# Attention's inverse sums as a scaled identity in a product, and two more weight pieces summed by VectorE

## The chip, the cores and the metric

One core of one Trainium2 chip. The metric is device microseconds of one execution. Below, PE is TensorE's matmuls, PEld its weight loads, DVE is VectorE, ACT ScalarE, POOL GpSimd and SP SyncE.

## The reference

Two layers of a diffusion backbone on 256 latent tokens of width 2048, with 256 context tokens. Layer 0 mixes by attention (16 heads of 128, 4 key heads), layer 1 by a Fourier transform; an MLP follows each. What matters here is layer 0's attention and the vectors from c that scale and shift:

```python
mod_lat = (silu_c @ ada_w[i] + ada_b[i])[:, None, :]
sh1, sc1, g1, sh2, sc2, g2 = jnp.split(mod_lat, N_MOD, axis=-1)
...
logits = jnp.concatenate([
    jnp.einsum('bqkgd,bskd->bkgqs', q, k_lat),
    jnp.einsum('bqkgd,bskd->bkgqs', q, k_ctx)], axis=-1).astype(jnp.float32) * scale
p = jax.nn.softmax(logits, axis=-1).astype(v_lat.dtype)
return (jnp.einsum('bkgqs,bskd->bqkgd', p[..., :s], v_lat)
        + jnp.einsum('bkgqs,bskd->bqkgd', p[..., s:], v_ctx))
...
x = x + g2 * sq_relu_mlp(modulate(rms_norm(x, norm_mlp_g[i]), sh2, sc2), mlp_w1[i], mlp_w2[i])
```

## The kernel before

The program is written out by hand for each engine: each engine's queue runs in the order of the code, and semaphores tie the queues. Weights come from HBM in pieces of 1 MB on SP's queue; ScalarE makes the high part of each slice (w_hi, L727) and VectorE the low part (w_lo, L1201), and a product with them is three matmuls (L1848 to L1850). This is done LOOKAHEAD = 4 slices ahead of TensorE.

**The attention loop** is the loop over n = 0 to 37 on each of three engines. Tile n is head n // 2 and token half n % 2, so there are 32 tiles of 128 queries by 512 keys. In step n TensorE issues, in this order: the score of tile n + 1 (L2204, one f32 product of 512 columns); from n = 6 a unit of the output projection W_o (block_unit, L1848 to L1850); an early piece, if the step has one (L1933); for m = n - 1 the four transposes of prob (L2242); at even n from 4 the four products of v with probT, for both tiles of head (n - 4) // 2 (L2257); and at n = 1, 3, 7, 9, 11 and 13 the turns of q_acc (L1963), which wait for VectorE's rotation of these heads (q_epilogue). VectorE takes the maximum of each score (L1523), then, with the exponent's sum from ScalarE (L937), inverts the sum (L1529) and multiplies the 128x512 tile prob by it (L1530), for tile m = n - 1. TensorE transposes the result, ScalarE copies it to probT (L926). Behind the products ScalarE and VectorE split the head's output in a high (L948) and a low part (h_lo, L1544) for block_unit. ScalarE also copies the turned heads to qT (L842).

**The early pieces.** The vector products silu(c) times ada_w for the first MLP's shift (v = 1, pieces j = 0 to 15) and scale (v = 2, j = 16 to 31) are done piece by piece, 1 MB each, from a ring of buffers that POOL's queue fills (load_vector, i = j + 16). A piece is either a group of four matmuls into bank 2 by TensorE (early_piece) or two halves of a running sum by VectorE (early_sum, L1505 for the first piece, L1508 for the rest). EARLY_TENSOR and EARLY_VECTOR say which. At the end early_fold adds VectorE's sum into the same bank. Of the scale vector's 16 pieces TensorE has j = 17 (at n = 25) and j = 19 (at n = 27). The vector sums of v = 2 begin at n = 23 with piece 16, and go on in the output projection behind the loop, at slice i of LATE_SUMS. A load may start once the piece that was in its buffer is used (before_early), and POOL's queue issues loads strictly in order.

Of the kernel before, what the change touches and what calls it, by code (L numbers as in the profile page):

```python
# [22 lines left out]
F32 = mybir.dt.float32  # L23
F32R = mybir.dt.float32r
ALU = mybir.AluOpType
# [3 lines left out]
P = 128  # L29
# [121 lines left out]
def early_slot(j):  # L151
# [1 line left out]
    return (4, 5, 7, 2, 7, 2, 10, 10, 0, 2, 1, 8, 0, 9, 1, 8)[j] if j < 16 else (9, 0, 8, 1)[j % 4]  # L153


EARLY_TENSOR = ((0, 1, 2, 3, 4, 5, 6, 7, 8, 10, 12, 14), (17, 19))
EARLY_VECTOR = ((9, 11, 13, 15), (16, 18, 20, 22, 24, 26, 28, 21, 23, 30, 25, 27, 29, 31))
LATE_SUMS = {3: ((21, 0), (21, 1)), 4: ((23, 0),), 5: ((23, 1),), 6: ((30, 0),), 7: ((30, 1),), 8: ((25, 0),), 11: ((25, 1),),
             12: ((27, 0),), 13: ((27, 1),), 14: ((29, 0),), 15: ((29, 1),), 16: ((31, 0),), 19: ((31, 1),)}


# [15 lines left out]
def vector_halves(j):  # L177

    return 2 * (EARLY_VECTOR[0] + EARLY_VECTOR[1]).index(j) + 2

# [64 lines left out]
def layer_block(nc, x, c, ctx_in, c_ctx, ada_w, ada_b, norm_mix_g, norm_mlp_g, w_qkv, q_g, k_g, w_o,  # L245
# [4 lines left out]
    def place(name, shape, dt, at):  # L250
        return nc.alloc_sbuf_tensor_at(name, shape, dt, offset=at)
# [11 lines left out]
    shared = base[0]  # L263
# [62 lines left out]
    probT = place("probT", [P, 2, 4, T], F32, shared + 24576)  # L326
    prob = place("prob", [P, 3, 2 * T], F32, shared + 32768)
    nmax = place("nmax", [P, 32, 4], F32, shared + 38912)
    sum_front = place("sum_front", [P, D], F32, shared)
    sum_down = place("sum_down", [P, D], F32, shared + 36864)  # L330

# [205 lines left out]
    def turned_bank(m):  # L537
        return 3 if m >= 5 and m % 2 else 6
# [101 lines left out]
    @block.gpsimd  # L640
    def _(pool):
        def load_start(n):

            if n >= 7:
                pool.wait_ge(ada_mm, n - 2)
            if n == 4:
                pool.wait_ge(ctx_rows_in, 16)
            if n < 8:
                dst, src = ring(start_slot(n)).rearrange("p (k c) -> p k c", k=8), first_v[n // 4, n % 4 // 2, n % 2]
            else:  # L650
                dst, src = ring(start_slot(n)).rearrange("p (k c) -> p k c", k=4), start_v[n // 8, n % 8 // 4, n % 4]
            pool.dma_start(dst, src).then_inc(ada_in[start_slot(n)], 16)

        def load_vector(i):

            lay, m = SUMS[i // KT]
            if i < 2:
                pool.wait_ge(prod_done, 32)
            elif i == 8:
                pool.wait_ge(ada_mm, 32)  # L660
            elif i == 9:
                pool.wait_ge(ada_mm, 30)
            elif i < 16:
                pool.wait_ge(ada_used, i - 1)
            elif i < 18:
                pool.wait_ge(prod_done, 64)
            elif i == 18:
                pool.wait_ge(ada_used, 7)
            elif i == 19:
                pool.wait_ge(ada_mm, 31)  # L670
            elif i < 22:
                pool.wait_ge(ada_mm, tensor_count(i - 18))
            elif i == 22:
                pool.wait_ge(prod_done, 80)
            elif i == 23:
                pool.wait_ge(ada_mm, tensor_count(6))
            elif i in (24, 26):
                pool.wait_ge(ada_used, 15 + (i - 24) // 2)
            elif i == 25:
                pool.wait_ge(ada_mm, tensor_count(5))  # L680
            elif i in (27, 29):
                pool.wait_ge(head_T, 11 + (i - 27) // 2)
            elif i < 50:
                j = before_early(i - 16) if i < 48 else 29 + 2 * (i - 48)
                if j in EARLY_VECTOR[j // KT]:
                    pool.wait_ge(early_used, vector_halves(j))
                else:
                    pool.wait_ge(ada_mm, tensor_count(j))
            else:
                pool.wait_ge(ada_used, i - 33)  # L690
            if i in (9 * KT, 9 * KT + 1):
                pool.wait_ge(slice_done, 2 * P_DOWN[0] - QKV + 128)
            pool.dma_start(ring(vector_slot(i)), ada_v[lay][m, i % KT]).then_inc(ada_in[vector_slot(i)], 16)  # L693

        for n in range(19):
            load_start(n)
        load_vector(0)
        load_vector(1)
        for a in range(6):
            load_start(19 + 2 * a)  # L700
            load_start(20 + 2 * a)
            load_vector(2 + a)
        load_start(31)
        for i in (8, 9, 16, 17, 10, 11, 18, 12, 19, 20, 21, 13, 14, 22, 23, 15):
            load_vector(i)
        for i in (*range(24, 41), 42, 44, 46, 41, 43, 45, *range(47, 160)):
            load_vector(i)


# [486 lines left out]
    def _(dve):  # L1196
# [322 lines left out]
        for n in range(38):  # L1519
            if n < 32:  # L1520
                h, tt = n // 2, n % 2
                dve.wait_ge(score_ready, n + 1)
                step(nc.vector.tensor_reduce(nmax[:, n, 0:1], ps[:, 4 + n % 2, :], AX_X, ALU.max))  # L1523
                nc.vector.scalar_tensor_tensor(nmax[:, n, 1:2], nmax[:, n, 0:1], -1.0, q_rs[:, h, tt:tt + 1], ALU.mult,
                                               ALU.mult).then_inc(max_ready, 1)
            m = n - 1
            if 0 <= m < 32:
                dve.wait_ge(exp_ready, m + 1)
                step(nc.vector.reciprocal(nmax[:, m, 3:4], nmax[:, m, 2:3]))  # L1529
                nc.vector.tensor_scalar(prob[:, m % 3, :], prob[:, m % 3, :], nmax[:, m, 3:4], None, ALU.mult).then_inc(prob_ready, 1)  # L1530
            if n in (1, 2, 4):
                add_product(76 + (1, 2, 3)[n // 2])
            if n == 16:
                gate_add(0, 7)
            if n in WOVEN_SPLITS:
                split_lo(QKV + WOVEN_SPLITS.index(n))
            if n == 0:
                ada_step(0, 11)
            if n in ROTATE_AT:
                q_epilogue(1 + ROTATE_AT.index(n) // 2, ROTATE_AT.index(n) % 2)  # L1540
            if n >= 5 and n % 2 == 1 and n < 37:
                h = (n - 5) // 2
                dve.wait_ge(o_hi_ready, h + 1)
                nc.vector.tensor_tensor(h_lo[:, h, :], ps[:, 7, 0:T], h_hi[:, h, :].bitcast(F32), ALU.subtract).then_inc(o_ready, 1)  # L1544
            if n in (1, 3, 6, 10):
                ada_step(0, 12 + (1, 3, 6, 10).index(n))
            if n == 7:
                dve.wait_ge(q_root, 2)
                step(nc.vector.reciprocal(q_rs[:, 4:16, :], q_rs[:, 4:16, :]))
            if n == 24:  # L1550
                take_early(1)
            if 13 <= n < 21 or 23 <= n < 37:
                early_sum((9 if n < 21 else 6) + (n - 13) // 2 * 2, (n - 13) % 2)
        split_lo(59)

# [287 lines left out]
    def _(pe):  # L1843
# [80 lines left out]
        def early_piece(j):  # L1924

            slot, v = vector_slot(16 + j), j // KT
            pe.wait_ge(ada_in[slot], 16 * vector_count(16 + j))
            if j == 0:
                pe.wait_ge(acc_add, 45)
            if j == EARLY_TENSOR[1][0]:  # L1930
                pe.wait_ge(early_ready, 1)
            for b in range(4):
                ins = mm(ps[32 * b:32 * b + 32, 2, :], silu[:, j % KT, :], ring(slot)[:, 512 * b:512 * (b + 1)],  # L1933
                         start=(j == EARLY_TENSOR[v][0]), stop=False, skip_group_check=True)
            ins.then_inc(ada_mm, 1)

        def early_fold(v):

            pe.wait_ge(early_used, vector_halves(EARLY_VECTOR[v - 1][-1]))
            total = (spare[7], ada_sum)[v - 1]  # L1940
            for b in range(4):
                ins = mm(ps[32 * b:32 * b + 32, 2, :], ones[:, 0:32], total[:, 512 * b:512 * (b + 1)], start=False, stop=True,
                         skip_group_check=True)
            ins.then_inc(ada_mm, 1)

# [262 lines left out]
        for n in range(38):  # L2208
# [18 lines left out]
                early_fold(1)  # L2227
            if n == 23:
                early_cols(1)
            if n in (25, 27):  # L2230
                early_piece(n - 8)
            m = n - 1
            if 0 <= m < 32:
                pe.wait_ge(prob_ready, m + 1)
                if m >= 5:
                    pe.wait_ge(probT_out, m - 1)
                elif m >= 1:
                    pe.wait_ge(probT_out, m)
                else:
                    pe.wait_ge(head_T_out, 5)  # L2240
                for st in range(4):
                    ins = nc.tensor.transpose(ps[:, turned_bank(m), st * P:(st + 1) * P], prob[:, m % 3, st * P:(st + 1) * P], ident[:, :])  # L2242
                ins.then_inc(probT_ready, 1)
            if n == 15:
                pe.wait_ge(o_ready, 6)
# [209 lines left out]
```

## Time and profile before

| what | before |
|---|---|
| median of 3 runs | 2003.79 us (2003.05 to 2006.21) |
| the profiled execution, its own time | 2005.52 us |
| its span | 2003.6 us |
| TensorE busy | 1965.9 us |
| VectorE busy | 1391.5 us |
| ScalarE busy | 969.3 us |

The span runs from the first to the last instruction of the profiled execution; its own time is 1.9 us longer. Busy times overlap. The attention loop lies between about 250 and 376 us of the span, and the output projection W_o between 376 and 437.

### The profile page before, as it was taken

The page shows a single profiled execution, that of the slowest core. Times are in us where ns is not written, and L with a number is a line of the kernel's source. Part 1 is how long each engine was busy: PE and PEld are TensorE (multiplying, and loading weights), DVE is VectorE, ACT ScalarE, POOL GpSimd, SP SyncE. Part 2 cuts the span into 40 slices and gives each one's busy share as a digit, 9 for nine tenths or more (in the row PEclk, how much of TensorE's full clock was granted, in tenths as well). Part 3 has the DMA queues.
Part 4 walks back from the last instruction along what each step waited for, and adds up shares of the span by engine and source line. Part 5 has one row for each costly group of instructions (what it writes and reads, how often), then busy time and mean ns, then how long its engine had stood idle before and what let it go on. Part 6 is the DMA issues. An engine that isn't in the chain of part 4 may idle for free.

```text
span 2003.6 us, 24992 instructions
## 1 busy us (share of the span) xinstructions
PE 1965.9 (98%) x10188; PEld 1609.5 (80%) x10188; DVE 1391.5 (69%) x1424; ACT 969.3 (48%) x1265; POOL 110.9 (6%) x196
## 2 busy tenths in 40 slices
PE   6999989999999999999999999999999999999998
PEld 4677756778888888888888888788888888888886
DVE  3666998889867787788888675766666455555556
ACT  6432565455544455544444464555554454444444
POOL 1111001000000000000000000000000000000000
PEclk9999999999999999999999999999999999999999
DMA  9998768779989899799999626577776566555653
GB/s 359 338 378 319 277 257 297 272 252 323 353 293 348 313 360 364 262 367 363 355 395 383 219 85 193 175 252 253 257 251 220 187 192 210 189 192 198 218 190 126
DMA packets 152261, 542.80 MB, mean 271 GB/s; under 512 B 9393, under 2 KB 10577, under 8 KB 114641
## 3 DMA queue, kind: packets, MB, share of 16 engines
q1 hardware_dynamic: 119312, 335.77, 47.9%
q0 software_dynamic: 31744, 201.34, 27.1%
q10 hardware_dynamic: 1090, 4.09, 0.5%
q8 instruction: 81, 1.33, 0.3%
q14 instruction: 34, 0.28, 0.0%
HBM read 535.91 MB, written 2.10 MB: 269 GB/s over the span
## 4 chain that ended last, share of the span: by engine, by line
PE 94%; DVE 3%; ACT 1%; DMA 1%; issue 1%; POOL 0%; ACTq 0%; DVEq 0%; POOLq 0%
PE ps L2098 13%; PE ps L2036 12%; PE ps L2032 12%; PE ps L2035 11%; PE ps L2096 11%; PE ps L2099 6%; PE ps L1848 6%; PE ps L2095 6%; PE ps L1849 5%; PE ps L1850 5%; PE ps L2257 1%; PE ps L1913 1%; PE ps L2204 1%; DMA spare<-in_ada_w 1%; PE ps L2242 1%
## 5 line engine op out<-in xcount | busy, mean ns | idle before, releaser
L1201 DVE TENSOR_TENSOR w_lo<-raw,w_hi 128x1024 fp32r<-128x1024 f32 x616 | 749.5, 1223 | 467.9 <-ACT w_hi L727 467.6
L727 ACT ACTIVATE w_hi<-raw 128x1024 fp32r<-128x1024 f32 x616 | 649.4, 1059 | 845.7 <-PE ps L2036 345.8
L2098 PE MATMUL ps<-hh,w_hi 128*128 128x512 f32 x1088 | 427.5, 398 | 1.1 <-DVE hh L1627 1.1
L2032 PE MATMUL ps<-w_hi,hh 128*128 128x512 f32 x992 | 385.9, 389 | 0.0
L2036 PE MATMUL ps<-w_hi,hh 128*128 128x512 f32 x992 | 385.9, 389 | 0.0
L2035 PE MATMUL ps<-w_lo,hh 128*128 128x512 f32 x992 | 385.9, 389 | 0.0
L2096 PE MATMUL ps<-hh,w_hi 128*128 128x512 f32 x960 | 379.9, 396 | 0.0
L2099 PE MATMUL ps<-hh,w_lo 128*128 128x256 f32 x1088 | 302.9, 278 | 0.0
L2095 PE MATMUL ps<-hh,w_lo 128*128 128x256 f32 x960 | 267.5, 279 | 0.0
L2099 PEld LDWEIGHTS ps<-hh,w_lo 128*128 128x128 f32 x1088 | 205.7, 189 | 40.9
L2035 PEld LDWEIGHTS ps<-w_lo,hh 128*128 128x128 f32 x992 | 186.2, 188 | 38.9
L2032 PEld LDWEIGHTS ps<-w_hi,hh 128*128 128x128 f32 x992 | 186.2, 188 | 38.5
L2036 PEld LDWEIGHTS ps<-w_hi,hh 128*128 128x128 f32 x992 | 186.2, 188 | 38.4
L2098 PEld LDWEIGHTS ps<-hh,w_hi 128*128 128x128 f32 x1088 | 207.2, 190 | 11.2 <-issue 5.0
L2095 PEld LDWEIGHTS ps<-hh,w_lo 128*128 128x128 f32 x960 | 180.2, 188 | 43.7
L1229 DVE SCALAR_TENSOR_TENSOR ada_sum<-ada_raw,silu,ada_sum 128x2048 f32<-128x2048 f32 x83 | 194.7, 2346 | 2.7 <-DMA ada_raw<-in_ada_w 2.6
L1848 PE MATMUL ps<-w_hi,hh 128*128 128x512 f32 x448 | 190.8, 426 | 3.5 <-DVE hh L1351 1.6
L2096 PEld LDWEIGHTS ps<-hh,w_hi 128*128 128x128 f32 x960 | 179.9, 187 | 0.0
L1849 PE MATMUL ps<-w_lo,hh 128*128 128x512 f32 x448 | 175.8, 392 | 0.0
L1850 PE MATMUL ps<-w_hi,hh 128*128 128x512 f32 x448 | 175.2, 391 | 0.0
L693 POOL DMA_DIRECT2D ada_raw<-in_ada_w x132 | 70.5, 534 | 1138.3 <-DVE ada_sum L1229 584.3
L1848 PEld LDWEIGHTS ps<-w_hi,hh 128*128 128x128 f32 x448 | 84.5, 189 | 39.7 <-issue 14.4
(252 smaller groups left out, 1620.4 us busy)
## 6 DMA issues: line engine op xcount, KB each, us to landing
raw<-in_mlp_w SPq DMA_DIRECT2D x256, 1024.0 KB, 5.3
ada_raw<-in_ada_w POOLq DMA_DIRECT2D x151, 1024.0 KB, 6.2
spare<-in_ada_w POOLq DMA_DIRECT2D x29, 1024.0 KB, 6.6
raw<-in_attn_w_qkv SPq DMA_DIRECT2D x24, 1024.0 KB, 10.1
raw<-in_attn_w_o SPq DMA_DIRECT2D x16, 1024.0 KB, 5.7
raw<-in_fourier_w_o SPq DMA_DIRECT2D x16, 1024.0 KB, 5.1
g_row<-in_ada_w POOLq DMA_DIRECT2D x12, 1024.0 KB, 9.0
g_row<-gate_rows SPq DMA_DIRECT2D x48, 64.0 KB, 5.2
```

The lines of the kernel that those rows point to most:

```text
L727: act.activation(w_slot(s)[0], raw[:, piece % RAW, s % 2, :], ACT.Copy).then_inc(hi_ready, 1)
L1201: nc.vector.tensor_tensor(lo, raw[:, s // 2 % RAW, s % 2, :], hi.bitcast(F32), ALU.subtract).then_inc(lo_ready, 1)
L1848: mm(dst, w_h, m_h, start=start, stop=False, skip_group_check=True)
L1849: mm(dst, w_h, m_l, start=False, stop=False, skip_group_check=True)
L1850: return mm(dst, w_l, m_h, start=False, stop=stop, skip_group_check=True)
L2032: ins = mm(bank_of(tt, nb), h_hi[:, k % KT, tok], hi[:, cols], start=start, stop=False)
L2035: mm(bank_of(tt, nb), h_hi[:, k % KT, tok], lo[:, cols], start=False, stop=False)
L2036: return mm(bank_of(tt, nb), h_lo[:, k % KT, tok], hi[:, cols], start=False, stop=stop)
L2095: mm(ps[:, bank, 0:T], w_lo[:, s % SPLIT, w], h_hi[:, k, :], start=False, stop=False, skip_group_check=True)
L2096: ins = mm(both, w_hi[:, s % SPLIT, w], hh[:, k, :, :], start=False, stop=(k == KT - 1), skip_group_check=True)
L2098: mm(both, w_hi[:, s % SPLIT, w], hh[:, k, :, :], start=(k == 0), stop=False, skip_group_check=True)
L2099: ins = mm(ps[:, bank, 0:T], w_lo[:, s % SPLIT, w], h_hi[:, k, :], start=False, stop=(k == KT - 1), skip_group_check=True)
```

## The change

The tile prob is no longer multiplied by the inverse sums. VectorE instead multiplies the 128x128 identity by them (a diagonal matrix, `inverse`, three buffers), and TensorE's transpose of prob becomes a product of prob with that diagonal matrix, which turns and scales in one. The second part gives pieces 17 and 19 to VectorE, so that TensorE has no piece of the scale vector. Piece 17 is the first of that vector's sums, at n = 21 and 22; piece 19 is summed at slice 0 of W_o, behind the first split there. early_fold(2) starts its bank in place of piece 17, and waits for early_ready, as that piece did. On POOL's queue the load of j = 23 moves behind that of j = 30, since its buffer is now free only after piece 19's sum.

```diff
-EARLY_TENSOR = ((0, 1, 2, 3, 4, 5, 6, 7, 8, 10, 12, 14), (17, 19))
-EARLY_VECTOR = ((9, 11, 13, 15), (16, 18, 20, 22, 24, 26, 28, 21, 23, 30, 25, 27, 29, 31))
-LATE_SUMS = {3: ((21, 0), (21, 1)), ...
+EARLY_TENSOR = ((0, 1, 2, 3, 4, 5, 6, 7, 8, 10, 12, 14), ())
+EARLY_VECTOR = ((9, 11, 13, 15), (17, 16, 18, 20, 22, 24, 26, 28, 19, 21, 23, 30, 25, 27, 29, 31))
+LATE_SUMS = {0: ((19, 0), (19, 1)), 3: ((21, 0), (21, 1)), ...
...
+    inverse = place("inverse", [P, 3, P], F32, shared + 39424)
...
-        for i in (*range(24, 41), 42, 44, 46, 41, 43, 45, *range(47, 160)):
+        for i in (*range(24, 39), 40, 42, 44, 46, 39, 41, 43, 45, *range(47, 160)):
             load_vector(i)
...
-                nc.vector.tensor_scalar(prob[:, m % 3, :], prob[:, m % 3, :], nmax[:, m, 3:4], None, ALU.mult).then_inc(prob_ready, 1)
+                nc.vector.tensor_scalar(inverse[:, m % 3, :], ident[:, :], nmax[:, m, 3:4], None, ALU.mult).then_inc(prob_ready, 1)
...
-            if 13 <= n < 21 or 23 <= n < 37:
+            if n in (21, 22):
+                early_sum(17, n - 21)
+            elif 13 <= n < 37:
                 early_sum((9 if n < 21 else 6) + (n - 13) // 2 * 2, (n - 13) % 2)
...
-            if j == EARLY_TENSOR[1][0]:
-                pe.wait_ge(early_ready, 1)
...
             pe.wait_ge(early_used, vector_halves(EARLY_VECTOR[v - 1][-1]))
+            if v == 2:
+                pe.wait_ge(early_ready, 1)
...
-                ins = mm(ps[32 * b:32 * b + 32, 2, :], ones[:, 0:32], total[:, 512 * b:512 * (b + 1)], start=False, stop=True,
+                ins = mm(ps[32 * b:32 * b + 32, 2, :], ones[:, 0:32], total[:, 512 * b:512 * (b + 1)], start=(v == 2), stop=True,
...
-            if n in (25, 27):
-                early_piece(n - 8)
...
-                    ins = nc.tensor.transpose(ps[:, turned_bank(m), st * P:(st + 1) * P], prob[:, m % 3, st * P:(st + 1) * P], ident[:, :])
+                    ins = mm(ps[:, turned_bank(m), st * P:(st + 1) * P], prob[:, m % 3, st * P:(st + 1) * P], inverse[:, m % 3, :],
+                             start=True, stop=True)
```

How the order moves shows best in a few rows. First TensorE at n = 25 and 26, before: score, W_o unit, piece 17, four transposes, and the next step.

```order
L2204 MATMUL ps<-kT,qT 128x512
L1848 MATMUL ps<-w_hi,hh 128x512
L1849 MATMUL ps<-w_lo,hh 128x512
L1850 MATMUL ps<-w_hi,hh 128x512
L1933 MATMUL ps<-ada_raw,silu 32x512 x4
L2242 MATMUL ps<-ident,prob 128x128 x4
L2204 MATMUL ps<-kT,qT 128x512
L1848 MATMUL ps<-w_hi,hh 128x512
L1849 MATMUL ps<-w_lo,hh 128x512
L1850 MATMUL ps<-w_hi,hh 128x512
L2242 MATMUL ps<-ident,prob 128x128 x4
L2257 MATMUL ps<-probT,v_acc 128x256 x4
```

The same steps of the changed kernel, whose lines have moved by one to three:

```order
L2207 MATMUL ps<-kT,qT 128x512
L1851 MATMUL ps<-w_hi,hh 128x512
L1852 MATMUL ps<-w_lo,hh 128x512
L1853 MATMUL ps<-w_hi,hh 128x512
L2243 MATMUL ps<-inverse,prob 128x128 x4
L2207 MATMUL ps<-kT,qT 128x512
L1851 MATMUL ps<-w_hi,hh 128x512
L1852 MATMUL ps<-w_lo,hh 128x512
L1853 MATMUL ps<-w_hi,hh 128x512
L2243 MATMUL ps<-inverse,prob 128x128 x4
L2259 MATMUL ps<-probT,v_acc 128x256 x4
```

The piece (L1933) is gone, and what turned prob with ident now multiplies it with inverse. VectorE before, from the multiply of prob at n = 21 on, through n = 22:

```order
L1530 TENSOR_SCALAR prob<-prob,nmax 128x512
L1201 TENSOR_TENSOR w_lo<-raw,w_hi 128x1024
L1544 TENSOR_TENSOR hh<-ps,hh 128x256
L1523 TENSOR_REDUCE nmax<-ps 128x1
L1524 SCALAR_TENSOR_TENSOR nmax<-nmax,q_rs 128x1
L1529 RECIPROCAL nmax<-nmax 128x1
L1530 TENSOR_SCALAR prob<-prob,nmax 128x512
L1201 TENSOR_TENSOR w_lo<-raw,w_hi 128x1024
L1523 TENSOR_REDUCE nmax<-ps 128x1
```

And in the changed kernel:

```order
L1531 TENSOR_SCALAR inverse<-ident,nmax 128x128
L1202 TENSOR_TENSOR w_lo<-raw,w_hi 128x1024
L1545 TENSOR_TENSOR hh<-ps,hh 128x256
L1506 TENSOR_SCALAR ada_sum<-ada_raw,silu 128x1024
L1524 TENSOR_REDUCE nmax<-ps 128x1
L1525 SCALAR_TENSOR_TENSOR nmax<-nmax,q_rs 128x1
L1530 RECIPROCAL nmax<-nmax 128x1
L1531 TENSOR_SCALAR inverse<-ident,nmax 128x128
L1202 TENSOR_TENSOR w_lo<-raw,w_hi 128x1024
L1506 TENSOR_SCALAR ada_sum<-ada_raw,silu 128x1024
L1524 TENSOR_REDUCE nmax<-ps 128x1
```

The two halves of piece 17 (L1506) stand behind the h_lo of n = 21 and behind the split of n = 22. VectorE at the beginning of W_o before, from the splits of slices 59 to 61 on:

```order
L1201 TENSOR_TENSOR w_lo<-raw,w_hi 128x1024 x3
L1575 TENSOR_TENSOR gated_120<-ps,g_row 128x512
L1578 TENSOR_TENSOR x_tm<-x_tm,gated_120 128x512
L1201 TENSOR_TENSOR w_lo<-raw,w_hi 128x1024
L1575 TENSOR_TENSOR gated_120<-ps,g_row 128x512
```

And in the changed kernel:

```order
L1202 TENSOR_TENSOR w_lo<-raw,w_hi 128x1024 x2
L1509 SCALAR_TENSOR_TENSOR ada_sum<-ada_raw,silu,ada_sum 128x1024 x2
L1202 TENSOR_TENSOR w_lo<-raw,w_hi 128x1024
L1578 TENSOR_TENSOR gated_121<-ps,g_row 128x512
L1581 TENSOR_TENSOR x_tm<-x_tm,gated_121 128x512
L1202 TENSOR_TENSOR w_lo<-raw,w_hi 128x1024
```

The two halves of piece 19 (L1509) stand between the splits of slices 60 and 61.

## Rows read from the trace of the kernel before

**Rows 1.** The page: busy time, and the chain that ended last by engine.
```profile
PE 1965.9 (98%) x10188; PEld 1609.5 (80%) x10188; DVE 1391.5 (69%) x1424; ACT 969.3 (48%) x1265; POOL 110.9 (6%) x196
...
PE 94%; DVE 3%; ACT 1%; DMA 1%; issue 1%; POOL 0%; ACTq 0%; DVEq 0%; POOLq 0%
```
**Rows 2.** Windows: stretch, its length, busy us of each engine (instructions), granted clock, DMA.
```profile
249.70:267.80 18.10, 18.01 (x92) 10.95 (x91) 17.72 (x29) 10.32 (x37) 2.41 (x5) 1.00 0.79 291
267.80:300.20 32.40, 27.16 (x136) 16.99 (x135) 30.92 (x61) 22.48 (x61) 2.90 (x6) 1.00 0.64 235
300.20:361.20 61.00, 60.96 (x304) 39.61 (x303) 50.30 (x104) 34.48 (x72) 8.05 (x14) 1.00 0.83 301
361.20:376.00 14.80, 13.38 (x61) 9.77 (x60) 12.64 (x21) 6.93 (x14) 1.58 (x3) 1.00 0.63 231
378.00:434.00 56.00, 56.00 (x249) 46.37 (x248) 49.67 (x48) 25.26 (x33) 2.64 (x5) 1.00 0.83 290
```
**Rows 3.** Groups by shape, 249.7 to 376: count, busy us, mean ns, idle before.
```profile
L2204 PE MATMUL ps<-kT,qT 128*128 128x512 f32 x64 | 32.9, 596 | 0.0
L2257 PE MATMUL ps<-probT,v_acc 128*128 128x256 f32 x128 | 30.3, 379 | 0.0
...
L2257 PEld LDWEIGHTS ps<-probT,v_acc 128*128 128x128 f32 x128 | 23.1, 190 | 2.6
...
L2242 PE MATMUL ps<-ident,prob 128*128 128x128 f32 x128 | 20.0, 279 | 3.5 <-ACT probT L926 2.5 <-DVE prob L1530 0.8
...
L1530 DVE TENSOR_SCALAR prob<-prob,nmax 128x512 f32<-128x512 f32 x32 | 15.6, 486 | 1.1
...
L1505 DVE TENSOR_SCALAR ada_sum<-spare,silu 128x1024 f32<-128x1024 f32 x2 | 1.5, 747 | 0.0
```
**Rows 4.** The chain in order of time: start, us on the chain, what.
```profile
340.70 0.79 PE ps L1951 x8
...
350.38 0.44 PE ps L2242 x4
350.82 1.73 PE ps L2257 x8
352.55 0.86 PE ps L2204 x2
```
**Rows 5.** Waits of TensorE, 255 to 300.2: us in total, times, longest.
```profile
PE ps L2242 <- ACT probT L926: 2.5, 1, 2.5
PE ps L1963 <- issue: 2.4, 2, 1.3
```
**Rows 6.** Timeline of ScalarE at the end of n = 3: start, us, idle before.
```profile
268.04 0.60 ACT L842 ACTIVATE qT<-ps 128x512 f32<-128x512 f32 x1 [0.88 <-PE ps L1963]
```
**Rows 7.** Timeline of TensorE: the scores that begin n = 27 to 30.
```profile
352.38 1.02 PE L2204 MATMUL ps<-kT,qT 128*128 128x512 f32 x2
...
355.52 1.02 PE L2204 MATMUL ps<-kT,qT 128*128 128x512 f32 x2
...
359.25 1.02 PE L2204 MATMUL ps<-kT,qT 128*128 128x512 f32 x2
...
361.24 1.02 PE L2204 MATMUL ps<-kT,qT 128*128 128x512 f32 x2
```
**Rows 8.** POOL's timeline (load of piece 17), and its loads' median landing, 230 to 460.
```profile
325.64 0.69 POOL L693 DMA_DIRECT2D ada_raw<-in_ada_w  x1
...
ada_raw<-in_ada_w POOLq DMA_DIRECT2D x18, 1024.0 KB, 7.2
```
**Rows 9.** Timeline of VectorE at n = 21.
```profile
333.48 0.42 DVE L1544 TENSOR_TENSOR hh<-ps,hh 128x256 fp32r<-128x256 f32 x1
```
**Rows 10.** Timeline of VectorE in W_o: first split, and piece 23's first half.
```profile
380.86 1.23 DVE L1201 TENSOR_TENSOR w_lo<-raw,w_hi 128x1024 fp32r<-128x1024 f32 x1 [0.97 <-ACT w_hi L727]
...
393.70 1.28 DVE L1508 SCALAR_TENSOR_TENSOR ada_sum<-ada_raw,silu,ada_sum 128x1024 f32<-128x1024 f32 x1
```
**Rows 11.** Waits of TensorE, 300.2 to 376.
```profile
PE ps L2242 <- DVE prob L1530: 0.8, 1, 0.8
```

More of the change, by code:

```diff
@@ L153, in early_slot @@
     return (4, 5, 7, 2, 7, 2, 10, 10, 0, 2, 1, 8, 0, 9, 1, 8)[j] if j < 16 else (9, 0, 8, 1)[j % 4]
-EARLY_TENSOR = ((0, 1, 2, 3, 4, 5, 6, 7, 8, 10, 12, 14), (17, 19))
-EARLY_VECTOR = ((9, 11, 13, 15), (16, 18, 20, 22, 24, 26, 28, 21, 23, 30, 25, 27, 29, 31))
-LATE_SUMS = {3: ((21, 0), (21, 1)), 4: ((23, 0),), 5: ((23, 1),), 6: ((30, 0),), 7: ((30, 1),), 8: ((25, 0),), 11: ((25, 1),),
+EARLY_TENSOR = ((0, 1, 2, 3, 4, 5, 6, 7, 8, 10, 12, 14), ())
+EARLY_VECTOR = ((9, 11, 13, 15), (17, 16, 18, 20, 22, 24, 26, 28, 19, 21, 23, 30, 25, 27, 29, 31))
+LATE_SUMS = {0: ((19, 0), (19, 1)), 3: ((21, 0), (21, 1)), 4: ((23, 0),), 5: ((23, 1),), 6: ((30, 0),), 7: ((30, 1),), 8: ((25, 0),), 11: ((25, 1),),
              12: ((27, 0),), 13: ((27, 1),), 14: ((29, 0),), 15: ((29, 1),), 16: ((31, 0),), 19: ((31, 1),)}
```

## The prediction, written before the changed kernel was run

> **What bounds the kernel now.** I began with the page. TensorE is busy for 98% of the span, and of the chain of work that ended last 94% is TensorE and 3% VectorE [rows 1]: a microsecond of TensorE's work is nearly always one of the span, unless it falls where TensorE waits. The change lies in the attention loop and behind it, so I cut that part into stretches. From 249.7 to 267.8 us (n = 0 to 3) TensorE is idle for 0.09 us, from 267.8 to 300.2 (n = 4 to 11) for 5.24, from 300.2 to 361.2 (n = 12 to 29) for 0.04, in the tail up to 376 for 1.42, and in W_o (378 to 434) for nothing. VectorE is idle for 1.9 us in the first two stretches, 10.7 in the third and 6.3 in W_o [rows 2]. So the loop has a first part in which VectorE, ScalarE and TensorE wait for each other, and a long second part that TensorE alone paces.
>
> Then I read the operations by shape. The 128 transposes of prob (32 tiles of 4) have 128 records. The 32 score products have 64, and the 64 products of prob and v have 128 [rows 3]: an ordinary f32 product is two records, a transpose is one. A record's mean duration (279 to 596 ns) is latency, since records overlap, so I took the pace from the chain in order of time: four transposes 0.44 us, eight records of probT times v (256 columns) 1.73, two of a score (512 columns) 0.86, eight with only 4 columns 0.79 [rows 4]. That is 0.11, 0.216 and 0.43 us per record for 128, 256 and 512 columns, in proportion, and a floor of 0.10 for a record whose columns are few but whose weights are a full 128x128.
>
> **The change part by part.**
>
> *Product in place of transpose, on TensorE.* Each of the 32 tiles issues four f32 products of 128 columns, with prob as weights and the scaled identity moving. By the count of records that is eight in place of four. By columns each takes 0.11, and the floor for full weights is no higher, so a tile costs 8 x 0.11 = 0.88 against 0.44: **+0.44**. The bounds are 0 (were it one record, as now) and +1.08 (were the weight load, 0.19 us for such products [rows 3], not overlapped: 8 x 0.19 - 0.44). The eight 4-column records also load full weights and take 0.79 in all, which puts it near the lower of the two.
>
> The Trainium skill speaks against the change here: FP8 and Floating Point Precision, TensorE Precision Notes, has true fp32 as four passes, and TensorE: Matmul & The Clock Gate, Terms, calls transpose mode 4x faster for FP32. The trace has a factor of two between transpose and product of equal columns, and the measurement decides.
>
> *First part, n = 1 to 11, 11 tiles.* They add 11 x 0.44 = 4.84 us to TensorE, and what counts is which of its waits they fill. These are 2.5 us for ScalarE's probT at n = 4, 2.4 us in two waits ahead of the turns of q_acc at n = 7 and 11 (for VectorE's rotation) [rows 5], and 0.3 that are left of the 5.24 idle, at n = 6. The first fills nothing: ScalarE reaches that copy only after one of qT for which it waited 0.88 us on TensorE's turns at the end of n = 3 [rows 6], so TensorE's delay goes round through ScalarE and comes back. The others (2.7) are filled, for TensorE arrives at them some 2 us late and VectorE does not. That leaves 4.84 - 2.7 = **+2.1**. The bounds: +4.84 if nothing is filled, and -2.4 if VectorE alone sets the pace there and its gain (below) is all that counts, 12 steps of 0.2.
>
> *VectorE's product.* The 128x512 tensor_scalar (0.486 us, 32 times) becomes 128x128, which the trace doesn't have. Between 128x512 and 128x1024 (0.747) [rows 3] the slope is 0.51 ns a column, which gives 0.29. The bounds are 0.49 (no gain) and 0.12 (a quarter of the present time, in proportion to the columns). I take 0.29: 0.2 less a step, 6.4 in all. In the second part this is worth nothing, for TensorE does not wait there.
>
> *Second part, n = 12 to 28, 17 tiles.* 17 x 0.44 = **+7.5**, hidden by nothing.
>
> *Pieces 17 and 19.* Between the starts of the scores lie 3.14 us at n = 27, which has a piece, and 1.99 at n = 29, the same step without one [rows 7]. So a piece is 1.15, and two are **-2.3**. Their sums go to VectorE: two halves at n = 21 and 22 (as the first of the vector they are tensor_scalar at 0.75, and piece 16's become the dearer form, about 1.28, as the sum at 393.70 [rows 10]), and two of 1.28 behind the first split of W_o. In the loop that is +2.6 us against 10.7 of idle, and 3.6 saved there; in W_o it is +2.6 against 6.3. Behind the new sums queue the next splits, for which TensorE would wait, but they are made several slices ahead; without that cover the 2.6 would be on the path.
>
> Piece 17 must land earlier now. It is issued at 325.64 and the median landing takes 7.2 us, so it is there near 332.9 [rows 8]; the sum wants it when the h_lo of 333.48 is done [rows 9], at 333.8 to 333.9. The tiles of the three steps between give about 1 us more. I cost it at nothing; were it 2 us late, VectorE's idle time would hide half and it would cost 1. On POOL's queue piece 23's load now waits for piece 19's second half, near 384.6 (380.86 + 1.2 + 2.5), and lands 7.2 later, near 391.8; its sum comes at 393.70 or after [rows 10], so it is in time.
>
> *Tail, n = 29 to 32, 4 tiles.* Here prob of the last tile comes 0.8 us after TensorE wants it [rows 11], behind an early sum. The four tiles add 1.8; that wait, less the 0.2 that VectorE is earlier, and a share of the other idle time of this stretch (1.42 in all) take 1.0 of it: **+0.8**.
>
> Sum: 2.1 + 7.5 - 2.3 + 0.8 = +8.1 us. The profiled execution took 2005.52 (span 2003.6), so it would take 2013.6. It lies 1.7 over the median of the runs, on which I put the forecast: 2003.79 + 8.1 = **2011.9 us**, slower by 0.4%. Everything behind the loop is paced by TensorE and only shifts.
>
> **The rivals.**
> - *A. The product runs at the transpose's pace*, one record each. For it: same shape and an identity as moving operand. Against it: every other f32 product has two records. Then TensorE gets nothing, the pieces give -2.3, the first part -1.6 through VectorE and the tail -0.2: -4.1, 1999.7 us, faster. It decides when the extra of a tile is below about 0.1 us.
> - *B. VectorE paces the first part.* For it: it is idle for only 1.9 of 50.5 us there. Against it: TensorE's idle time is in a few waits, and n = 8 to 10 have hardly any. -2.4 instead of +2.1: +3.6, 2007.4, at the edge of no change.
> - *C. The weight load is not overlapped*: 1.08 a tile, 0.64 over my price on the 28 tiles that count: +18 more, 2030. Against it: the 4-column row.
> - *D. A product is four times a transpose*: 1.76 a tile instead of 0.88, 0.88 more on 28 tiles: +25, 2037. Against it: the score's 0.86 for 512 columns is 1.68 ns a column, twice the transpose's 0.86. The skill's 4x (TensorE: Matmul & The Clock Gate, Terms) would be this case.
>
> **How the numbers follow.** Mine 0.78, B 0.08, A 0.07, C 0.04, D 0.03. A difference under 0.2% (4.0 us) is about what a measurement of this kernel can't tell from none. Faster is A, 0.07; within 0.2% are B and a corner of mine, 0.10; slower is the rest, 0.83. Mine alone spans +5 to +11.7 (waits of the first part and of the tail filled or not: +2.8 and +1.0 above the sum; more filled, 3 below it). With B's edge the range is 2007.0 to 2015.5.
>
> **What would show it.** 256 records for the product, with chain pieces of 0.87 to 0.90 us for eight; scores 2.4 us apart at n = 25, 27 and 29, and 4.2 at the even steps; the wait for probT at n = 4 still there, those ahead of the turns of q_acc gone; W_o without idle time on TensorE; VectorE's product near 0.29. I am wrong if the product has 128 records, if n = 12 starts no later than 300.2, or if VectorE waits for ada_raw at n = 21.

## The result, and the profile after

| what | before | after |
|---|---|---|
| median, timed side by side | 2004.53 us (4 runs, 2003.05 to 2006.21) | 2014.45 us (4 runs, 2013.59 to 2015.39) |
| the profiled execution, its own time | 2005.52 us | 2014.73 us |
| its span | 2003.6 us | 2012.6 us |

The changed kernel is slower: ratio 1.0048, 95% interval 1.0036 to 1.0061, that is 7 to 12 us, about 9.6. The forecast was 2011.9 us in a range of 2007.0 to 2015.5.

First the page of the changed kernel, busy time and the chain by engine (before in [rows 1]):

```profile
PE 1977.1 (98%) x10300; PEld 1625.7 (81%) x10300; DVE 1390.0 (69%) x1428; ACT 970.7 (48%) x1265; POOL 110.0 (5%) x196
...
PE 95%; DMA 3%; DVE 1%; ACT 0%; issue 0%; POOL 0%; SPq 0%; ACTq 0%; DVEq 0%; POOLq 0%
```

TensorE has 112 records more (128 for the product, less 16 of the two pieces) and 11.2 us more busy time. VectorE's busy time is nearly the same: what its short product saves, the four new half sums take.

The windows of the changed kernel, cut at the same steps as [rows 2] (n = 0 to 3, 4 to 11, 12 to 28, tail, W_o; same columns):

```profile
249.20:268.50 19.30, 19.30 (x104) 12.54 (x103) 18.91 (x30) 10.30 (x37) 2.51 (x5) 1.00 0.74 273
268.50:302.80 34.30, 31.80 (x169) 22.50 (x167) 28.62 (x63) 22.83 (x61) 2.62 (x5) 0.95 0.60 222
302.80:367.20 64.40, 64.40 (x347) 46.77 (x346) 46.90 (x100) 33.97 (x70) 6.84 (x13) 1.00 0.73 263
367.20:384.70 17.50, 16.79 (x85) 13.14 (x85) 13.71 (x23) 7.96 (x16) 1.59 (x3) 1.00 0.63 228
387.00:443.00 56.00, 56.00 (x248) 46.39 (x248) 51.65 (x50) 25.38 (x32) 3.17 (x6) 1.00 0.86 303
```

From n = 12 on TensorE is idle for nothing up to the tail, as before, and W_o has no idle time either. New is the granted clock of 0.95 in the second row.

Where the time came: between the first score of the loop (249.17) and the last product of v (382.69) lie 133.52 us, before 124.31 (249.67 to 373.98). The loop has 9.2 us more. Everything behind it nearly only shifts: the transposes of x behind W_o start 8.68 us later than before, TensorE's last product 9.04 (2003.38 and 1994.34).

Groups by shape in the loop (count, busy us, mean ns, idle before; before in [rows 3]):

```profile
L2243 PE MATMUL ps<-inverse,prob 128*128 128x128 f32 x256 | 35.7, 284 | 2.7 <-ACT probT L927 2.5 <-DVE inverse L1531 0.2
L2243 PEld LDWEIGHTS ps<-inverse,prob 128*128 128x128 f32 x256 | 33.4, 195 | 12.9 <-issue 9.7 <-DVE inverse L1531 1.5
...
L1531 DVE TENSOR_SCALAR inverse<-ident,nmax 128x128 f32<-128x128 f32 x32 | 9.2, 287 | 1.1
```

256 records stand where the transpose had 128. The chain in order of time gives their pace, as [rows 4] did:

```profile
296.27 0.89 PE ps L2243 x8
297.16 1.73 PE ps L2259 x8
298.89 0.86 PE ps L2207 x2
```

Eight records take 0.89 us, 0.45 more than the four of the transpose. The scores that begin n = 25 to 29 (before in [rows 7]) are 2.45, 4.17, 2.45, 4.18 us apart:

```profile
354.00 1.02 PE L2207 MATMUL ps<-kT,qT 128*128 128x512 f32 x2
356.45 1.02 PE L2207 MATMUL ps<-kT,qT 128*128 128x512 f32 x2
360.62 1.02 PE L2207 MATMUL ps<-kT,qT 128*128 128x512 f32 x2
363.07 1.02 PE L2207 MATMUL ps<-kT,qT 128*128 128x512 f32 x2
367.25 1.02 PE L2207 MATMUL ps<-kT,qT 128*128 128x512 f32 x2
```

All of TensorE's waits from 250 to 310 (before in [rows 5]): the one for probT is left, those ahead of the turns of q_acc are gone.

```profile
PE ps L2243 <- ACT probT L927: 2.5, 1, 2.5
```

And its waits from 310 to 390 (before in [rows 11]): the 0.8 us for prob is down to 0.2.

```profile
PE ps L1851 <- DVE hh L1545: 0.5, 2, 0.2
PE ps L2243 <- DVE inverse L1531: 0.2, 1, 0.2
```

VectorE at n = 21: the h_lo, and the first half of piece 17 right behind it. The second row has no wait in brackets, so piece 17 was there. The third row is its load on POOL's queue, which landed 9.2 us later.

```profile
339.29 0.42 DVE L1545 TENSOR_TENSOR hh<-ps,hh 128x256 fp32r<-128x256 f32 x1 [0.30 <-ACT hh L949]
339.63 0.74 DVE L1506 TENSOR_SCALAR ada_sum<-ada_raw,silu 128x1024 f32<-128x1024 f32 x1
...
329.93 0.53 POOL L694 DMA_DIRECT2D ada_raw<-in_ada_w  x1
```

### The profile page after: what moved, and what is told of

Same layout as the page of the kernel before. It is cut to its first block, busy times and chain, and to the rows that moved or that the text cites. A ratio compares the mean times of both kernels' runs of the same rounds, so it can differ in the third digit from the quotient of the medians.

```text
span 2012.6 us, 25224 instructions
## 1 busy us (share of the span) xinstructions
PE 1977.1 (98%) x10300; PEld 1625.7 (81%) x10300; DVE 1390.0 (69%) x1428; ACT 970.7 (48%) x1265; POOL 110.0 (5%) x196
## 4 chain that ended last, share of the span: by engine, by line
PE 95%; DMA 3%; DVE 1%; ACT 0%; issue 0%; POOL 0%; SPq 0%; ACTq 0%; DVEq 0%; POOLq 0%
PE ps L2101 13%; PE ps L2035 11%; PE ps L2038 11%; PE ps L2039 11%; PE ps L2099 11%; PE ps L2102 6%; PE ps L1851 6%; PE ps L1852 6%; PE ps L1853 6%; PE ps L2098 6%; PE ps L2243 2%; PE ps L2259 1%; PE ps L2207 1%; PE ps L1916 1%; DMA g_row<-in_ada_w 1%; DMA c_rows<-in_ctx 1%
## 5 line engine op out<-in xcount | busy, mean ns | idle before, releaser
L2101 PEld LDWEIGHTS ps<-hh,w_hi 128*128 128x128 f32 x1088 | 207.3, 191 | 11.2 <-issue 5.0
L1853 PE MATMUL ps<-w_hi,hh 128*128 128x512 f32 x448 | 174.7, 390 | 0.0
```

What stands on the lines that cost most here:

```text
L1853: return mm(dst, w_l, m_h, start=False, stop=stop, skip_group_check=True)
L2101: mm(both, w_hi[:, s % SPLIT, w], hh[:, k, :, :], start=(k == 0), stop=False, skip_group_check=True)
```

## The experiments

My theory after the result: the whole loss is 0.45 us per tile for the second record of each product, less the waits it fills in the first part and less 2.4 us for the two pieces. The rivals: that moving the pieces brought nothing and the product cost less; that VectorE's shorter product is what fills the waits; and that the 0.95 clock is part of the change.

Each profile was cut at the starts of the scores, as in the prediction: first part from the loop's first score to that of n = 12, second part up to that of n = 29, tail up to the last product of v. The column clock tells whether the granted clock fell in the first part of that profile. Ratios are to the kernel before, timed beside each.

| kernel | first | second | tail | loop | clock | median us | ratio (95%) |
|---|---|---|---|---|---|---|---|
| before | 50.56 | 59.02 | 14.73 | 124.31 | full | 2004.53 | 1 |
| before again (e6) | 50.88 | 59.04 | 14.72 | 124.64 | fell | 2003.79 (1 run) | |
| changed | 53.63 | 64.45 | 15.44 | 133.52 | fell | 2014.45 | 1.0048 (1.0036 to 1.0061) |
| changed again (e10) | 52.13 | 64.45 | 15.45 | 132.03 | full | 2013.61 | 1.0048 (1.0035 to 1.0060) |
| product alone (e1) | 53.77 | 66.83 | 15.43 | 136.03 | fell | 2015.51 | 1.0048 (1.0034 to 1.0061) |
| pieces alone (e2) | 50.90 | 57.74 | 15.46 | 124.10 | fell | 2005.85 | 1.0001 (0.9992 to 1.0009) |
| short VectorE product, transposes kept (e3) | 49.96 | 58.78 | 14.33 | 123.07 | fell | 2003.56 | 0.9985 (0.9976 to 0.9994) |
| changed, pieces 4 and 5 at n = 4 (e4) | 51.85 | 64.46 | 15.43 | 131.74 | full | 2012.22 | 1.0033 (1.0021 to 1.0046) |
| before + both piece moves (e8) | 51.23 | 57.73 | 15.45 | 124.41 | fell | 2005.37 | 0.9997 (0.9988 to 1.0005) |
| before + pieces 4 and 5 at n = 4 (e9) | 50.59 | 59.02 | 14.72 | 124.33 | full | 2006.07 | 1.0002 (0.9993 to 1.0010) |
| one-pass product (e7) | 48.80 | 57.12 | 14.86 | 120.78 | full | 2002.87 | 0.9986 (0.9977 to 0.9995) |
| one-pass, pieces left (e11) | 49.92 | 59.20 | 14.38 | 123.50 | fell | 2003.17 | 0.9984 (0.9975 to 0.9993) |
| one-pass, earlier copy (e12) | 48.78 | 57.12 | 14.85 | 120.75 | full | 2001.91 | 0.9981 (0.9972 to 0.9990) |
| changed, earlier copy (e13) | 50.64 | 64.45 | 15.43 | 130.52 | full | 2011.68 | 1.0035 (1.0022 to 1.0047) |

A step of the second part or the tail repeats from profile to profile within 0.02 us, while the ratios of the medians carry an interval of 1.7 to 2.5 us to either side. So a part's size is read from the traces, and the sign of the whole from the medians.

### One part of the change at a time

**The product alone**: the scaled identity and the product, with pieces 17 and 19 left on TensorE.

```diff
-                nc.vector.tensor_scalar(prob[:, m % 3, :], prob[:, m % 3, :], nmax[:, m, 3:4], None, ALU.mult).then_inc(prob_ready, 1)
+                nc.vector.tensor_scalar(inverse[:, m % 3, :], ident[:, :], nmax[:, m, 3:4], None, ALU.mult).then_inc(prob_ready, 1)
...
-                    ins = nc.tensor.transpose(ps[:, turned_bank(m), ...], prob[:, m % 3, ...], ident[:, :])
+                    ins = mm(ps[:, turned_bank(m), ...], prob[:, m % 3, ...], inverse[:, m % 3, :], start=True, stop=True)
```

> Only the first half of the change: scaled identity and product, with pieces 17 and 19 left to TensorE at n = 25 and 27. Theory 1 (a tile costs TensorE 0.45 us, a piece 1.15): 2.3 us more than the full change, so 11 to 12.5 us over before, with the steps at n = 25 and 27 at 3.6 us between scores instead of 2.45. Rival (the pieces on VectorE cost as much as they save, since its sums delay something): within 1 us of the full change, some 9.5 to 10 over before.

Timeline, the scores that begin n = 25 to 28, 3.64, 4.18 and 3.64 us apart:

```profile
353.66 1.02 PE L2205 MATMUL ps<-kT,qT 128*128 128x512 f32 x2
357.30 1.02 PE L2205 MATMUL ps<-kT,qT 128*128 128x512 f32 x2
361.48 1.02 PE L2205 MATMUL ps<-kT,qT 128*128 128x512 f32 x2
365.12 1.02 PE L2205 MATMUL ps<-kT,qT 128*128 128x512 f32 x2
```

n = 25 and 27 take 1.19 us more each than the 2.45 of the full change, so there the two pieces give 2.4. The second part is 7.81 us longer than before (17 steps of 0.46) and 2.38 longer than with the pieces moved. The medians, 2015.51 and 2014.45, have equal ratios and don't resolve that difference.

**The pieces alone**: the tables, the load order and early_fold as in the change, prob multiplied and transposed as before.

```diff
-EARLY_TENSOR = ((0, 1, ..., 12, 14), (17, 19))
+EARLY_TENSOR = ((0, 1, ..., 12, 14), ())
```

> Only the second half: pieces 17 and 19 summed by VectorE, prob still multiplied in full and transposed. Theory 1: TensorE loses 2 x 1.15 us in a part of the loop that it alone paces, VectorE hides the sums: 2.0 to 2.4 us under before (0.1%). Rival (VectorE without the short product becomes the pace from n = 21 on): between 0 and 1.5 us under before, with new waits of TensorE for prob at n = 22 to 29.

Its scores that begin n = 25 to 29 (n = 28, at 353.64, is left out):

```profile
345.42 1.02 PE L2207 MATMUL ps<-kT,qT 128*128 128x512 f32 x2
347.41 1.02 PE L2207 MATMUL ps<-kT,qT 128*128 128x512 f32 x2
351.64 1.02 PE L2207 MATMUL ps<-kT,qT 128*128 128x512 f32 x2
...
357.85 1.02 PE L2207 MATMUL ps<-kT,qT 128*128 128x512 f32 x2
```

And its wait for prob among TensorE's waits from 310 to 390 (0.8 in [rows 11]):

```profile
PE ps L2243 <- DVE prob L1531: 2.1, 4, 0.8
```

The steps n = 25 and 27 fall to 1.99 as they should (-2.3), but n = 26 and 28 rise from 3.7 to 4.2 (+1.0) and the tail by 0.7: in steps of 1.99 us TensorE catches up with VectorE and waits for prob. Of 2.3 us some 0.5 are left in the trace (124.10 against the 124.64 of the other profile of before with a fallen clock), and nothing that the runs can tell (ratio 1.0001). The pieces are worth 2.3 only where something else slows TensorE, and in this change the product does.

**The short VectorE product with the transposes kept**: VectorE makes `inverse` as in the change, but nothing reads it, and the transposes turn the undivided prob. The output lacks the division by the sums; the time is that of the other operations.

```diff
-                nc.vector.tensor_scalar(prob[:, m % 3, :], prob[:, m % 3, :], nmax[:, m, 3:4], None, ALU.mult).then_inc(prob_ready, 1)
+                nc.vector.tensor_scalar(inverse[:, m % 3, :], ident[:, :], nmax[:, m, 3:4], None, ALU.mult).then_inc(prob_ready, 1)
```

> VectorE makes the scaled identity (128x128), but nothing reads it: TensorE transposes prob as before, so the output lacks the division by the sums. Pieces as before. It takes the product's price away and leaves VectorE's gain. Theory 1: worth something only where TensorE waits for VectorE, that is at n = 7 and 11, at the tail, and n = 20: 1.5 to 3 us under before. Rival B of the prediction (VectorE paces the whole first part): its 12 steps give 2.4, and the tail 0.4 more, and the waits ahead of the turns of q_acc remain. If it paced the loop as a whole: 6.4 under.

Groups of the transposes and of VectorE's product:

```profile
L2243 PE MATMUL ps<-ident,prob 128*128 128x128 f32 x128 | 20.1, 281 | 3.1 <-ACT probT L927 2.5 <-DVE inverse L1531 0.6
...
L1531 DVE TENSOR_SCALAR inverse<-ident,nmax 128x128 f32<-128x128 f32 x32 | 9.2, 287 | 1.1
```

Against the profile of before with a fallen clock: first part -0.92, second -0.26, tail -0.39. The waits ahead of the turns of q_acc are 1.0 us here in place of 1.6. The first part gained less than the 2.4 us that rival B had for it. So VectorE's part of the change is a gain (0.9985, the interval is clear of 1), and what the product adds on TensorE is the distance from here to the product alone: +3.8, +8.05 and +1.1 us by part, 13 in the trace and 12 in the medians (2015.51 - 2003.56).

### The granted clock at n = 4

The 0.95 of the changed kernel's second window comes from one place. The same window of 4 us in three profiles (columns as in [rows 2]), first the changed kernel:

```profile
272.00:276.00 4.00, 3.93 (x15) 3.61 (x16) 2.81 (x8) 3.21 (x13) 0.00 (x0) 0.60 0.02 6
```

The kernel before, in its second profile (e6):

```profile
272.00:276.00 4.00, 4.00 (x13) 2.56 (x12) 3.63 (x10) 3.31 (x16) 0.00 (x0) 0.58 0.00 0
```

The kernel before, in its first:

```profile
272.00:276.00 4.00, 3.89 (x17) 2.32 (x15) 3.86 (x10) 4.00 (x21) 0.00 (x0) 1.00 0.00 0
```

Ahead of it stands the 2.5 us wait for probT. Timeline of TensorE at n = 4 in the changed kernel:

```profile
268.54 1.02 PE L2207 MATMUL ps<-kT,qT 128*128 128x512 f32 x2
272.07 2.04 PE L2243 MATMUL ps<-inverse,prob 128*128 128x128 f32 x8 [2.50 <-ACT probT L927]
273.91 2.56 PE L2259 MATMUL ps<-probT,v_acc 128*128 128x256 f32 x8
276.30 1.02 PE L2207 MATMUL ps<-kT,qT 128*128 128x512 f32 x2
```

The same rows in its second profile (e10), where n = 4 begins at 269.98:

```profile
273.51 1.13 PE L2243 MATMUL ps<-inverse,prob 128*128 128x128 f32 x8 [2.51 <-ACT probT L927]
274.48 1.89 PE L2259 MATMUL ps<-probT,v_acc 128*128 128x256 f32 x8
276.21 1.02 PE L2207 MATMUL ps<-kT,qT 128*128 128x512 f32 x2
```

> The kernel before once more, one look. In four profiles (the change, its halves, the short vector product) TensorE's granted clock fell behind the wait for probT at n = 4, and step n = 4 took 1.6 to 1.7 us longer; in the one profile of the kernel before it did not, with the same wait of 2.5 us. Theory 1 (the fall is a matter of when the wait comes in an execution, and the kernel before has it too in a part of its executions): step n = 4 takes 7.4 us instead of 5.7 here, or stays at 5.7, and either way the wait is 2.5 us. Rival (the kernel before is spared, so the clock belongs to the change): 5.7 us again, as the halves and the short vector all were not.

> The changed kernel once more, beside the three that follow. By my account it stands at +0.4 to +0.5% over before (some +9 us), and the granted clock falls to half for about 3.4 us at n = 4 in its profile, behind the 2.5 us wait for probT, so that n = 4 takes 7.7 us. If that fall is an accident of one execution, n = 4 takes 6.1 here and the time is 1.6 us nearer to before.

With the same wait, the eight products take 1.84 us from start to start in one profile and 0.97 in the other, and n = 4 takes 7.76 and 6.23. The kernel before has both cases too, and there the fall costs only 0.3 us (first part 50.88 against 50.56): n = 4 and 5 are 1.7 longer, and n = 6 and 7 shorter by 1.4, because TensorE had waits at the turns of q_acc that take it up. In the changed kernel the product has filled these, and the fall costs 1.5 in full (53.63 against 52.13). So the profile of after overstates the change's own cost in the loop: like with like it is 132.03 - 124.31 = +7.7 us with a full clock, or 133.52 - 124.64 = +8.9 with a fallen one. In the medians this doesn't show: the ratio of the second measurement of the changed kernel (e10) is 1.0048 again.

**Filling the wait**: the changed kernel, with the early pieces 4 and 5 at n = 4 in place of n = 2. The same edit on before alone is e9, and on before with pieces 17 and 19 moved it is e8.

```diff
-            if n == 2:
+            if n == 4:
                 early_piece(4)
                 early_piece(5)
```

> The full change, with TensorE's early pieces 4 and 5 moved from n = 2 to n = 4, ahead of the wait for probT there. Theory 1 (the wait of 2.5 us at n = 4 comes from ScalarE's chain, and the lower granted clock behind it costs 1.6 us more): the pieces (1.9 us) fill the wait and the clock stays up: 1.9 + 1.6 = 3.5 us under the full change, 6 to 7 over before. Rival (the clock falls whatever TensorE does before, or the delay goes round through ScalarE and the wait only moves): 0 to 2 us under the full change, and the stretch from 268 to 300 us still shows a granted clock under 1.00.

Timeline of TensorE, the products with the inverse at n = 2 and n = 4:

```profile
263.13 1.13 PE L2243 MATMUL ps<-inverse,prob 128*128 128x128 f32 x8 [1.56 <-ACT probT L927]
...
272.58 1.13 PE L2243 MATMUL ps<-inverse,prob 128*128 128x128 f32 x8 [0.65 <-ACT probT L927]
```

The two pieces (1.8 us) fill the wait at n = 4 down to 0.65, and leave one of 1.56 at n = 2 where they had been. The clock stays full in this one profile, so it is 1.8 us under the profile with the fall, but only 0.3 under e10: the wait was moved, not removed. The other two:

> The kernel before with one edit: TensorE's pieces 4 and 5 at n = 4 instead of n = 2. Theory 1: worth only the clock in those executions in which it falls (1.6 us), and a little of the wait: 0.5 to 2 us under before, granted clock 1.00 from 260 to 290. Rival (the wait of 2.5 us is filled): 2 to 4 us under before. Third (VectorE's pace in the first part hides it): no change.

> Transposes and the full product on VectorE as before; pieces 17 and 19 to VectorE, and TensorE's pieces 4 and 5 from n = 2 to n = 4. With the pieces alone TensorE waited 0.5 us for prob at n = 26 and again at 28, and the clock fell at n = 4, so that nothing was left of 2.3 us. Theory 1: the clock stays up, 1.3 us are left of the pieces, the fill itself only moves the wait to n = 2: 1.5 to 3 us under before. Rival (ScalarE's chain loses what the fill gives): within 1 us of before.

Before with the fill: loop 124.33, as before, ratio 1.0002. With both: 124.41, ratio 0.9997; here the clock fell one wait earlier, behind 1.9 us without work at n = 2. Neither gives anything.

**The copy that is late**: ScalarE copies the turned tile 2 to probT at n = 3, ahead of the turned q, instead of at n = 4 behind it and all that follows it. Here on the changed kernel (e13); the same on the one-pass kernel is e12.

```diff
         for n in range(38):
-            if 2 <= n < 7:
+            if 2 <= n < 7 and n != 4:
                 turned_out(n - 2)
...
+            if n == 3:
+                turned_out(2)
             if n in HEADS_AT:
                 heads_out(6 + HEADS_AT.index(n), 7)
```

> The changed kernel (f32 product) with the same earlier copy of tile 2. TensorE's waits of the first part behind n = 4 are filled in it already, so a wait removed at n = 4 should be all gain: 2.5 us for the wait, and 1.6 for the clock that falls behind it if the wait is what lets it fall, some 4 us under the changed kernel, so +0.2 to +0.3% over before. Rival: ScalarE's later copy of the turned q delays the products that need it, and the gain is 0 to 1.5 us; then the score of n = 4 or 5 waits for qT.

Timeline of TensorE in n = 4 and 5, from the products of v:

```profile
271.20 1.89 PE L2261 MATMUL ps<-probT,v_acc 128*128 128x256 f32 x8
273.21 1.12 PE L2209 MATMUL ps<-kT,qT 128*128 128x512 f32 x2
274.96 1.13 PE L2245 MATMUL ps<-inverse,prob 128*128 128x128 f32 x8 [0.62 <-ACT probT L927]
```

The wait at n = 4 is gone (that step takes 3.76 us, 6.23 in e10), and 1.0 of it comes back at n = 5, which takes 2.72 in place of 1.75, for the next copy. The gain is 1.5 us against the profile with a full clock and 3.0 against that with the fall, and 1.9 in the medians timed side by side (2011.68, 2013.61): less than the 4 expected, since I had counted the fall as certain and no new wait. The rival's size (0 to 1.5) fits, its reason doesn't: TensorE never waited for qT.

### The second record of the product

**One pass**: the full change, with prob and inverse in F32R (their values rounded, so the result is less exact).

```diff
-    prob = place("prob", [P, 3, 2 * T], F32, shared + 32768)
+    prob = place("prob", [P, 3, 2 * T], F32R, shared + 32768)
...
-    inverse = place("inverse", [P, 3, P], F32, shared + 39424)
+    inverse = place("inverse", [P, 3, P], F32R, shared + 39424)
```

> The full change with prob and the scaled identity in fp32r, so that the product of a tile is four records instead of eight; both are rounded to fp32r, which is less exact. Theory 1 (the price of the change is the number of records of 0.11 us each): 128 records, at most 0.44 us a tile on the chain: 10 us or more under the full change in the loop (all 32 tiles lose 0.45 us, the first part less), 3 to 5 us under before. Rival (the price is that of a product's weight load or start, whatever the type): 4 to 8 us over before. If a record of 128 columns in fp32r takes the time of its columns alone (0.053 us), 6 us more would go, down to VectorE's pace.

Groups of the product in this kernel:

```profile
L2243 PE MATMUL ps<-inverse,prob 128*128 128x128 f32 x128 | 19.6, 275 | 3.4 <-ACT probT L927 2.5 <-DVE inverse L1531 0.9
L2243 PEld LDWEIGHTS ps<-inverse,prob 128*128 128x128 f32 x128 | 18.0, 190 | 14.5 <-issue 9.6 <-DVE inverse L1531 3.4
```

Its chain in order of time in the second part, from the first of three records of 512 columns in F32R to the product's four:

```profile
341.25 0.23 PE ps L1851
...
341.94 0.39 PE ps L2243 x4
```

128 records, as the transpose had, and the step n = 25 takes 1.95 us, the transpose's 1.99. The loop is 3.5 us shorter than before and 11.3 shorter than the changed kernel's with a full clock; the ratio is 0.9986. That settles the cause: with one record the change is a gain, with two a loss. The edit changes the type too, but a record of 128 columns takes 0.10 us here and 0.11 in f32, so it is the count that differs. It also shows a floor: a 512-column record in F32R takes 0.23 us, so 128 columns would need 0.06 by proportion, and four 0.23, but they take 0.39. With full weights no record shown here comes under about 0.1 us (0.39 / 4, and 0.79 / 8 for the 4-column ones of [rows 4]).

**One pass, pieces 17 and 19 left on TensorE.**

> The product with prob and inverse in F32R (less exact), but pieces 17 and 19 left on TensorE. If two pieces are worth their 2.3 us whatever the product costs, this is 2.3 us over the one-pass kernel with the pieces moved (near 2005.1 where that has 2002.9, so within 0.1% of before). If the pieces' room is given back in waits for VectorE, as it was when they were moved alone, the two one-pass kernels are equal (2002.9), and steps n = 26 and 28 are shorter here by what n = 25 and 27 are longer (3.1 instead of 1.95).

The second part is 2.08 us longer than in the one-pass kernel, the tail 0.48 shorter. The difference in the first part is mostly the fall of the clock, which this profile has. So with a cheap product the two pieces are worth 1.6 us, between the 0.5 of before and the 2.4 of the full change; the medians (2003.17 and 2002.87, not timed side by side) don't tell them apart.

**One pass, earlier copy.**

> The one-pass product with one thing more: at n = 3 ScalarE copies the turned prob of tile 2 to probT ahead of the copy of the turned q, instead of behind it at n = 4. My account is that ScalarE's copy is late at n = 4 because it stands behind a copy that waits for TensorE's turns; then the 2.5 us wait for probT at n = 4 goes (under 0.8 is left), and the time falls by 1 to 2.5 us against the one-pass kernel. Rival: another wait of the first part (turns of q_acc, the inverse) takes what is gained, and n = 12 starts where it did, within 0.4 us.

All of TensorE's waits from 250 to 310 in the one-pass kernel:

```profile
PE ps L2243 <- ACT probT L927: 2.5, 1, 2.5
PE ps L1966 <- issue: 1.4, 2, 0.8
```

The same with the earlier copy:

```profile
PE ps L1968 <- issue: 1.7, 2, 1.1
PE ps L2245 <- DVE inverse L1533: 1.1, 1, 1.1
PE ps L1853 <- issue: 0.3, 1, 0.3
```

The rival was right: the 2.5 us for probT are gone, other waits stand in their place, and the first part is 48.78 against 48.80. The profile puts 1.1 us of them on VectorE's inverse. For the 2.0 ahead of the turns of q_acc (L1968) and of a unit of W_o (L1853) it names nobody; by the code TensorE waits there for VectorE's rotation and its h_lo. Its median of 2001.91 is the lowest of all and its ratio of 0.9981 clear of 1, but not of the one-pass kernel's 0.9986. These two and e11 beat both kernels, at the price of rounded factors. That less work for VectorE in the first part would bring more there is likely from these waits, but wasn't tried.

## Why the prediction was right

- **Product for transpose, +0.44 a tile: right.** 256 records, eight in 0.89 us, +0.45 to 0.46 a step. The count of records by kind of operation carried it. Rival A has 128 records, which only the one-pass kernel shows. For C it would take 1.52 a tile (measured 0.89; the load's 0.195 us is overlapped), for D 1.76. The Trainium skill's "4x faster for FP32" of transpose mode (TensorE: Matmul & The Clock Gate, Terms) is not what this trace has: the factor is 2 at these shapes. At 512 columns an f32 product does take nearly four times one in F32R (0.86 and 0.23 us); that the floor of 0.1 us a record holds up the transpose at 128 columns would fit both, but no run shows it.
- **Second part, +7.5 and -2.3: right.** It became +5.43, expected 5.2. The product alone adds 7.81, and the two pieces take off 2.38 of that. What I had not seen is that the 2.3 hangs on the product: alone, they give 0.5.
- **First part, +2.1: right in mechanism.** +1.57 at a full clock. The waits ahead of the turns were filled (n = 7 and 11 went from 3.92 and 4.90 us to 2.88 and 4.08, with 0.45 more work in each), the wait for probT stayed at 2.5. Of 4.95 us of new work 3.4 were taken up, not the 2.7 priced: 2.8 at the turns (priced at 2.4) and 0.5 at n = 6 (priced at 0.3; 5.41 us before, 5.37 now). The profile of after shows +3.07, with 1.5 for the fall of the clock, which the prediction didn't have.
- **Tail, +0.8: right**, +0.72. The wait for prob of 0.8 us went down to 0.2. Without the product the two pieces alone lengthen the tail as much (+0.73), by waits for prob, and so does the product alone (+0.70): the two halves don't add up here.
- **VectorE's product, 0.29 us: right**, 0.287. Alone with transposes it gains 1.6 in the trace, near the 1.8 that rival A gave it in the first part and the tail (-1.6 and -0.2).
- **Loads: right, with less room than expected.** The load of piece 17 took 9.2 us to land, not 7.2, and was there near 339.1 (329.93 + 9.2); its sum began 0.5 us later, without a wait on VectorE (0.2 in e10, where the load took 9.5), while the prediction had nearly 2 us to spare. I had used the median of all these loads; piece 17's own took 8.0 us in the kernel before. W_o has no idle time on TensorE.
- **Rival B, VectorE paces the first part: wrong here**, since most of TensorE's steps there grew by 0.35 to 0.5 (all but n = 6, 7 and 11). The one-pass kernel comes near it: its first part is 1.8 us under before, against B's 2.4, and a wait taken away at n = 4 came back as others.
- **The sum**: +8.1 expected; the loop gained 7.7 at a full clock, 9.2 between the two profiles as they are, 9.6 by the ratio (7 to 12). The forecast is 2.5 us under the median of 2014.45; 0.7 of that is the median of before, which came out at 2004.53 and not 2003.79, and the rest is within what the runs can tell. The range has a small slip: 8.1 + 2.8 + 1.0 is 11.9, not 11.7.

What stays open: how often the clock falls in the timed runs, and so how much of 9.6 it makes. Of nine profiles with the whole 2.5 us wait at n = 4 it fell in six, in both kernels.

## What to carry to other kernels

Moving a scale from VectorE into TensorE's identity is free only if the product stays one record; count the records of the transpose and of an ordinary product of the same type in the trace before, and multiply by the pace of a record on the chain. A saving on an engine that sets the pace ends where the next engine catches up: the same two pieces were worth 0.5, 1.6 or 2.4 us, by how much slack VectorE had. A wait that a profile shows may be the cushion of another: price it by what stands behind it, and take a second profile before a cost of 1 or 2 us is put down to a change.

## What the runs showed of the hardware

- **The granted clock can fall to half behind a wait of 2.5 us**, in one execution and not in the next of the same kernel (windows of 4 us from 0.57 to 0.73, or 1.00). It is half, 1.2 GHz, by the eight products that took 1.84 us in place of 0.97. The slow stretch costs TensorE 1.5 to 1.7 us, less what the waits behind it take up. That such a drop comes after idle time and to half rate is what the Trainium skill has (TensorE: Matmul & The Clock Gate, Part 1); the profiles with two waits of 1.6 and 0.65 us (e4), without one over 1.1 (e12) or without one over 0.7 (e13) had none, one with 1.9 us (e8) had one and one with the same 1.9 (e9) had none. With one profile for each of these, no run shows that a shorter wait keeps the clock up.
- **A record of 128 columns in F32R is hardly faster than a transpose's of the same size**, 0.10 against 0.11 us, though by its columns alone it would take 0.06.
- **A 128x128 tensor_scalar takes 287 ns, a 128x512 one 486**, so a quarter of the columns is 59% of the time.
